# Expert weights in a ring of eight 16 KB blocks: one change to a one-core encoder step

## The chip, the cores and the metric

The kernel runs on one core of one Trainium2 chip. The metric is the time on the device, in microseconds (us), of the one core. Before the change three runs took 1047.72, 1048.99 and 1050.06 us, median 1048.99. The engines are named as in the profile: PE is TensorE, DVE is VectorE, ACT is ScalarE, POOL is GpSimd and SP is SyncE, whose queue issues most of the transfers.

## What is computed

One layer over 1104 rows (64 of a sample stream, 16 meta rows and 1024 of a prompt), model width 1024, all in 32 bit:

```python
h = x + W_out [ PoolMix(u) ; RMSNorm_head(GLA(q, k, v, alpha)) * silu(r) ]
    where [u, q, k, v, r, z] = RMSNorm(x) @ W_in
h = h + HierMoE(RMSNorm(h))        # top-1 group of 4, then top-2 of its 8 experts
y = RMSNorm(h)
# one expert:
h_e = silu(xb @ w_eg[e]) * (xb @ w_eu[e]); y_e = h_e @ w_ed[e]
```

GLA is a gated linear attention in chunks of 64 rows, PoolMix a mean over the last 2, 4, 8 or 16 rows. There are 32 experts. Each has three weight matrices of 2 MB (gate 1024x512, up 1024x512, down 512x1024), 201 MB together, and each is loaded once.

## The kernel before

**Tiles.** The rows, padded, are cut in nine tiles of 128 tokens. The *front* (the mixer) goes through them on PE one by one: tile 0 and tile 1 are written out, tiles 2 to 7 are a loop, and tile 8 is written out again. A tile's PE work is, in this order: z, q and k, then u, r, v (`proj_z`, `proj_qk_gate`, `proj_u`, `proj_r`, `proj_v`; products in L1422 and L1474), the pooling, the attention, and the output product of the tile before (L1543). The last tile's output product has two halves, and each half counts up the semaphore `pe_half_out`. All weights of the front stay in one tensor, `arena`, of 24 Ki elements per partition: first `w_in` (2064 columns by 8), then `w_out`.

**Experts.** Behind the last tile the 32 experts run, each for up to 88 gathered rows. For each expert PE computes gate and up (`up`, L1713, 256 matmuls) and down (`down`, L1725 and L1732). ACT and DVE make the hidden values between them (L804, L1237 to L1243), ACT copies the result out (L809, L813), and POOL gathers rows from `hn_rows` in memory (L556) and scatters results into `pick_rows` (L567). DVE transposes the gathered rows (L1207). Experts alternate between two sets of buffers.

**Weights.** There are two sets of three weight buffers, `wg`, `wu` and `wd`, each a 16 KB block per partition of `arena`, at the places of `starts` (L212). Expert e uses set e mod 2. The buffers lie on weights of the front, so they can only be filled when these are no longer read. SP's program does that in `load_weights` (L456): the first three loads and the fourth wait for the last tile's v product (`pe_v`), the fifth for `pe_half_out` at 2 and for the last store of `hn_rows`, the sixth for the gathered rows of expert 1. From expert 2 on each load waits for the product two experts earlier that read the same block.

**Order.** The order of the work is written by hand. Each engine runs its own program, and semaphores tie them together. SP's queue is in order: a load that waits holds up all loads behind it. PE's expert code is experts 0 and 1 written out, a loop over pairs (L1763), and experts 30 and 31 written out. Behind the first tiles and next to experts 0 to 2, DVE also builds the tables of where each result row lies (`slots`, L1261), and a small copy of the last 15 pooling rows, `pool_out` (L1226), is stored; PE's up product of expert 0 waits for it, because it clears the PSUM bank.

**The tail.** When all results are in memory SP loads them back, PE and DVE add them to `h`, and the last norm is applied (L1363, L1795 to L1804).

## Time and profile before

| what | before |
|---|---|
| median of 3 runs | 1048.99 us |
| the profiled execution | 1047.59 us |
| its span | 1045.7 us |
| PE busy | 994.2 us (95%) |
| DVE busy | 561.9 us (54%) |
| ACT busy | 243.9 us (23%) |
| POOL busy | 106.1 us (10%) |
| moved by DMA | 263.23 MB, mean 252 GB/s |
| chain that ended last | PE 66%, DMA 28%, DVE 4% |

The span is the time between the first and the last instruction that the profiler saw; the execution lasts 1.9 us longer. A busy share of PE counts a matmul as busy while it is in the pipeline, so 95% is not a measure of how well PE is used. The chain goes backwards from the last instruction to what released it, and its shares add up over stages with different limits: DMA's 28% all lie in the second half. A stage has to be looked at by itself, with the windows (busy time of each engine in a stretch), the timeline of one queue, and the DMA issues of a short window, which give the time from issue to landing. The granted clock of TensorE was at its full level in all stretches of the experts.

### The profile page before, as it was taken

Reading aid. Unit: us, or ns where it says so; the run is one execution under the profiler, and the core shown is the slowest. Engines: PE = TensorE matmul, PEld = TensorE weight load, DVE = VectorE, ACT = ScalarE, POOL = GpSimd, SP = SyncE. Lnnn points to the kernel's source line nnn. Section 1 sums busy time; section 2 is a strip of 40 time slices with the busy share of each in tenths; the row PEclk is TensorE's granted clock in tenths of the full one; section 3 lists DMA queues with packets and bytes.
Section 4 is the critical chain, followed back from the end, with each engine's and each line's share of the span. In section 5 each row is a group of like instructions: output and inputs, shape, how many; then the busy total and the mean of one; then the engine's idle time right before and its main releaser. Section 6 shows DMA issues by size and latency. Waiting matters only on the chain.

```text
span 1045.7 us, 33186 instructions
## 1 busy us (share of the span) xinstructions
PE 994.2 (95%) x14570; PEld 788.2 (75%) x14570; DVE 561.9 (54%) x1283; ACT 243.9 (23%) x531; POOL 106.1 (10%) x169
## 2 busy tenths in 40 slices
PE   7999999999999999999989999999999999999976
PEld 7786868686867677748778888788787787878842
DVE  2333534444444444427976766665756657566337
ACT  2352332323232323121111111111011110111125
POOL 0110101010101010101111011011011110111000
PEclk9999999999999999999999999999999999999989
DMA  9911010100000101175999999999999999999959
GB/s 328 337 72 41 1 41 0 40 0 40 0 40 0 40 0 40 35 328 179 410 418 424 417 425 419 420 421 416 426 415 419 421 415 424 415 419 420 384 189 387
DMA packets 54293, 263.23 MB, mean 252 GB/s; under 512 B 11368, under 2 KB 13992, under 8 KB 46026
## 3 DMA queue, kind: packets, MB, share of 16 engines
q1 hardware_dynamic: 43466, 235.12, 55.2%
q0 software_dynamic: 8192, 18.06, 4.5%
q10 hardware_dynamic: 2592, 9.44, 2.2%
q8 instruction: 32, 0.52, 0.2%
q14 instruction: 11, 0.09, 0.0%
HBM read 247.11 MB, written 27.19 MB: 262 GB/s over the span
## 4 chain that ended last, share of the span: by engine, by line
PE 66%; DMA 28%; DVE 4%; issue 1%; ACT 1%; SPq 0%; DVEq 0%; POOLq 0%; ACTq 0%
DMA arena<-in_w_ed 23%; PE bank L1422 19%; PE bank L1543 11%; PE bank L1713 11%; PE bank L1725 6%; PE bank L1474 6%; PE bank L1732 4%; DMA arena<-in_w_eg 3%; PE bank L1403 2%; PE bank L1523 1%; DVE hnT L1207 1%; DMA arena<-in_w_in 1%; PE bank L1481 1%; PE bank L1540 1%; PE bank L1802 1%
## 5 line engine op out<-in xcount | busy, mean ns | idle before, releaser
L1422 PE MATMUL bank<-xnT,arena 128*128 128x128 f32 x1728 | 201.1, 277 | 3.4 <-DMA arena<-in_w_in 2.0
L1422 PEld LDWEIGHTS bank<-xnT,arena 128*128 128x128 f32 x1728 | 196.9, 193 | 5.8 <-DVE sA L950 3.5
L1713 PEld LDWEIGHTS bank<-xnT,arena 128*64 128x64 f32 x4096 | 156.7, 137 | 10.9 <-DMA arena<-in_w_eg 7.0
L1713 PEld LDWEIGHTS bank<-hnT,arena 128*64 128x64 f32 x4096 | 156.3, 137 | 9.4 <-issue 5.2
L1713 PE MATMUL bank<-xnT,arena 128*64 128x88 f32 x4096 | 160.2, 240 | 3.2 <-DMA arena<-in_w_eg 1.9
L1713 PE MATMUL bank<-hnT,arena 128*64 128x88 f32 x4096 | 159.3, 239 | 2.3 <-DVE hnT L1216 1.6
L1543 PE MATMUL bank<-arena,mixT 128*128 128x512 f32 x256 | 111.7, 593 | 0.0
L1725 PE MATMUL bank<-arena,osq 128*32 128x384 f32 (+1 forms) x768 | 85.7, 487 | 14.4 <-DMA arena<-in_w_ed 12.3
L1237 DVE TENSOR_SCALAR mixT<-mixT 128x352 f32<-128x352 f32 x32 | 12.4, 388 | 147.5 <-ACT mixT L804 147.5
L1725 PE MATMUL bank<-arena,silu_r 128*32 128x384 f32 (+1 forms) x768 | 85.7, 487 | 6.2 <-DMA arena<-in_w_ed 4.2
L1543 PEld LDWEIGHTS bank<-arena,mixT 128*128 128x128 f32 x256 | 47.9, 190 | 57.2 <-issue 57.1
L1207 DVE STREAM_TRANSPOSE hnT<-xs 32x256 f32<-32x256 f32 x192 | 83.5, 435 | 6.2
L1732 PE MATMUL bank<-arena,silu_r 128*32 128x256 f32 (+1 forms) x384 | 86.1, 380 | 0.0
L1732 PE MATMUL bank<-arena,osq 128*32 128x256 f32 (+1 forms) x384 | 85.9, 380 | 0.0
L1207 DVE STREAM_TRANSPOSE xnT<-window_work 32x256 f32<-32x256 f32 x180 | 78.2, 434 | 5.2
L1238 DVE RECIPROCAL mixT<-mixT 128x352 f32<-128x352 f32 x32 | 75.3, 2353 | 1.1
L1474 PE MATMUL bank<-arena,xnT 128*128 128x512 f32 x144 | 64.8, 592 | 0.0
L809 ACT ACTIVATE kz_v<-bank 88x384 f32<-88x384 f32 x32 | 13.8, 482 | 172.3 <-PE bank L1732 172.3
L1732 PEld LDWEIGHTS bank<-arena,osq 128*32 128x32 f32 (+1 forms) x384 | 40.0, 107 | 16.3
L1732 PEld LDWEIGHTS bank<-arena,silu_r 128*32 128x32 f32 (+1 forms) x384 | 39.9, 107 | 16.5 <-issue 0.2
L809 ACT ACTIVATE hs<-bank 88x384 f32<-88x384 f32 x31 | 13.5, 483 | 162.2 <-PE bank L1732 162.2
L530 POOL TENSOR_TENSOR window_work<-window_work 128x568 f32<-128x568 f32 x9 | 10.2, 1135 | 397.3 <-ACT window_work L677 397.3
(260 smaller groups left out, 999.4 us busy)
## 6 DMA issues: line engine op xcount, KB each, us to landing
arena<-in_w_eg SPq DMA_DIRECT2D x32, 2048.0 KB, 26.9
arena<-in_w_eu SPq DMA_DIRECT2D x32, 2048.0 KB, 27.1
arena<-in_w_ed SPq DMA_DIRECT2D x32, 2048.0 KB, 26.7
hn_rows<-hs ACTq DMA_DIRECT2D x18, 512.0 KB, 3.4
arena<-pick_rows SPq DMA_DIRECT2D x18, 512.0 KB, 10.1
arena<-in_w_in SPq DMA_DIRECT2D x3, 2048.0 KB, 12.8
arena<-in_w_out SPq DMA_DIRECT2D x1, 4096.0 KB, 13.8
out_y_prompt<-arena SPq DMA_DIRECT2D x8, 512.0 KB, 6.2
```

What stands on the lines that cost most here:

```text
L809: A(ye[b][0:BLOCK, half * OWN:(half + 1) * OWN], bank[6 + half][0:BLOCK, 0:OWN], ACT.Copy).then_inc(s["ye_ready"], 1)
L1207: ins = V.transpose(slotsT[b][q:q + TG, :, a:a + TG], by_k[:, :, q:q + TG])
L1237: moe.then(V.tensor_scalar(gs[:, 0:NH], sig[:, 0:NH], 1.0, None, ALU.add))
L1238: moe.then(V.reciprocal(gs[:, 0:NH], gs[:, 0:NH]))
L1403: return nc.tensor.transpose(out, src, ident[0:n, 0:n])
L1422: last = mm(out, w_in_sb[:, k, a:b], xnT[:, k, :], start=k == 0, stop=k == KD - 1)
L1474: last = mm(bank[6][:, :], xnT[:, k, :], w_in_sb[:, k, V0:R0], start=k == 0, stop=k == KD - 1)
L1481: last = mm(bank[4][:, g * P:(g + 1) * P], w_pool_sb[:, g, :], pooled[:, g, :], start=True, stop=True)
L1543: return mm(out[:, :], mix[:, k, :], w_out_sb[:, k, n * 512:(n + 1) * 512], start=k == 0, stop=k == KD - 1)
L1713: last = mm(out[q * SW:(q + 1) * SW, n * BLOCK:(n + 1) * BLOCK], w[:, k, m * P + q * SW:m * P + (q + 1) * SW], rowsT[b][:, k, :], start=k ...
L1725: last = mm(bank[6 + half][a:z, 0:OWN], tokens(k, g), wd[b][:, k, half * OWN:(half + 1) * OWN], start=k == 0, stop=k == KF - 1)
L1732: return mm(bank[n][STORE:STORE + z - a, c:c + REST], tokens(k, g), wd[b][:, k, 2 * OWN:D], start=k == 0 and c == 0, stop=k == KF - 1, ski ...
```

## The change

The blocks get a new layout. `arena` becomes six blocks of 16 KB per partition (6 x `EW` elements). Two more blocks are made by laying small tensors of the front into `work` and `late`, two new tensors, with `part` and `carve`. The eight blocks form a ring: piece number 3e + kind (kind 0 gate, 1 up, 2 down) goes to place (3e + kind) mod 8. Each front weight gets a block of its own (q/k, u, r, v), and `w_out` fills two blocks, one for each half of its columns.

```diff
-        arena = sb("arena", [P, KD * D_IN + KD * D])
...
-        starts = {("g", 0): 0, ("u", 0): EW, ("d", 0): 2 * EW, ("g", 1): 3 * EW, ("u", 1): KD * D_IN, ("d", 1): KD * D_IN + EW}
...
+        arena = sb("arena", [P, 6 * EW])
+        work = sb("work", [P, EW])
+        late = sb("late", [P, D + EW])
...
+        blocks = [arena[:, n * EW:(n + 1) * EW] for n in range(6)] + [work[:, :], late[:, D:]]
...
+        w_qk_sb, w_u_sb, w_r_in_sb, w_v_sb = (by_k(blocks[n]) for n in range(4))
+        w_out_sb = arena[:, 4 * EW:].rearrange("p (h k n) -> p h k n", h=2, k=KD)
...
+        ring = [blocks[n] for n in (0, 1, 2, 3, 4, 6, 5, 7)]
+        RING = len(ring)
+        KINDS = 3
...
+        AROUND = RING
...
+            return divmod(KINDS * b + kind, RING)
```

In `work` lie `one_dv`, `w_pool_sb`, `z_sb`, `qk`, `q_wide`, `k_i`, `k_dec`, `sc`, `sB`, `pooled` and `er`; in `late` lie `w_up_sb`, both router weights, `gate_work`, `sA`, `s_sample` and the windows. The rows of the experts' first lane stay in the first part of `late`.

SP's loads change as follows. `load_freed` waits, for each piece, for the reader eight pieces earlier.

```diff
+            def load_freed(t, b):
...
+                e = AROUND * t + b
+                if not (isinstance(t, int) and e < 3):
+                    sp.wait_ge(s["pe_u2"], 2 * (e - 2))
+                    load_piece(t, b, 0)
+                    sp.wait_ge(s["pe_d"], e - 2)
+                    load_piece(t, b, 1)
+                sp.wait_ge(s["pe_g"], e - 1)
+                load_piece(t, b, 2)
+
+            sp.wait_ge(s["pe_qk"], TILES)
+            load_piece(0, 0, 0)
+            sp.wait_ge(s["pe_u"], TILES)
+            load_piece(0, 0, 1)
+            sp.wait_ge(s["pe_r"], TILES)
+            load_piece(0, 0, 2)
             sp.wait_ge(s["pe_v"], TILES)
-            load_weights(0, 0)
-            load_weights(0, 1)
+            load_piece(0, 1, 0)
             sp.wait_ge(s["sA_ready"], TILES)
             for p in range(PAIRS):
-                sp.dma_start(gla_prompt[2 * p:2 * p + 2].rearrange("h k v -> (h k) v"), sA[:, p, :]).then_inc(s["outs_stored"], 16)
+                sp.dma_start(gla_prompt[2 * p:2 * p + 2].rearrange("h k v -> (h k) v"), sA[:, p, :]).then_inc(s["states_stored"], 16)
+            sp.wait_ge(s["pe_half_out"], 1)
+            load_piece(0, 1, 1)
+            sp.wait_ge(s["own_rstd_ready"], 1)
+            load_piece(0, 1, 2)
+            sp.wait_ge(rows_in[0], 16)
+            sp.wait_ge(s["pe_half_out"], 2)
+            load_piece(0, 2, 0)
+            sp.wait_ge(s["pe_router"], TILES)
+            sp.wait_ge(s["states_stored"], 16 * 2 * PAIRS)
+            load_piece(0, 2, 1)
...
-            with sp.Fori(1, NE // 2) as t:
-                for b in range(2):
-
-                    sp.wait_ge(s["pe_g"], 2 * t + b - 1)
-                    load_weights(t, b)
+            for b in range(2, AROUND):
+                load_freed(0, b)
+            with sp.Fori(1, NE // AROUND) as t:
+                for b in range(AROUND):
+                    load_freed(t, b)
```

PE's experts are written out for one turn of eight and then run in a loop of eight, so that each has a fixed place in the ring:

```diff
-            expert(0, 0)
-            expert(0, 1)
-            with pe.Fori(1, NE // 2 - 1) as t:
-                expert(t, 0)
-                expert(t, 1)
-            expert(NE // 2 - 1, 0)
-            expert(NE // 2 - 1, 1, last=True)
...
+            for b in range(AROUND):
+                expert(0, b)
+            with pe.Fori(1, NE // AROUND) as t:
+                for b in range(AROUND):
+                    expert(t, b)
```

Four smaller edits go with the layout. The output weights come in two loads and are scaled on a strided view. `pool_out` now lies in `hs`, so DVE waits for the last store of `hn_rows` before it writes there, and ACT waits for the stores of `pool_out` before it works on expert 1. The slot tables move into constants that are no longer needed, where there is room for 18 of 25 columns, so one table takes two steps.

```diff
+            dve.wait_ge(s["hn_stored"], 16 * PICKS * TILES)
             for n in range(2):
                 V.tensor_copy(pool_out[n], bank[4 + 2 * n][0:HIST, :]).then_inc(s["pool_out_ready"], 1)
...
             expert(0, 0, True)
+            act.wait_ge(s["pool_stored"], 16 * 2)
             expert(0, 1, True)
...
+                for a in range(0, EXTRA, X_PART):
+                    n = min(X_PART, EXTRA - a)
...
-            sp.dma_start(w_out_sb, w_out.rearrange("(k p) n -> p k n", p=P)).then_inc(s["w_out_in"], 16)
+            for h in range(2):
+                sp.dma_start(w_out_sb[:, h, :, :], w_out.rearrange("(k p) n -> p k n", p=P)[:, :, h * 512:(h + 1) * 512]).then_inc(piece_in[(4, 6)[h]], 16)
```

SP's queue before, from the first expert load to the loop. `in_w_eg`, `in_w_eu` and `in_w_ed` are gate, up and down weights:

```order
L458 DMA arena<-in_w_eg 128x4096 [waits pe_v]
L464 DMA arena<-in_w_eu 128x4096
L469 DMA arena<-in_w_ed 128x4x1024
L458 DMA arena<-in_w_eg 128x4096
L464 DMA arena<-in_w_eu 128x4096 [waits hn_stored,pe_half_out]
L469 DMA arena<-in_w_ed 128x4x1024 [waits rows_in1]
L476 DMA out_gla_prompt<-sA 128x128 [waits sA_ready]
L476 DMA out_gla_prompt<-sA 128x128
L478 DMA out_pool_sample<-q_wide 15x512 [waits pool_out_ready]
L479 DMA out_pool_prompt<-sc 15x512
```

The same place of SP's queue in the changed kernel. A load into `late` or `work` is one into the two new blocks:

```order
L496 DMA arena<-in_w_eg 128x4096 [waits pe_qk]
L496 DMA arena<-in_w_eu 128x4096 [waits pe_u]
L496 DMA arena<-in_w_ed 128x4x1024 [waits pe_r]
L496 DMA arena<-in_w_eg 128x4096 [waits pe_v]
L519 DMA out_gla_prompt<-late 128x128 [waits sA_ready]
L519 DMA out_gla_prompt<-late 128x128
L496 DMA arena<-in_w_eu 128x4096 [waits pe_half_out]
L496 DMA work<-in_w_ed 128x4x1024 [waits own_rstd_ready]
L496 DMA arena<-in_w_eg 128x4096 [waits pe_half_out,rows_in0]
L496 DMA late<-in_w_eu 128x4096 [waits states_stored,pe_router]
L532 DMA out_pool_sample<-hs 15x512 [waits pool_out_ready]
L532 DMA out_pool_prompt<-hs 15x512
```

The first four loads now wait for four different products instead of one, two more loads (`in_w_eg` and `in_w_eu` of expert 2) stand ahead of the `pool_out` stores, and the two `gla_prompt` stores have moved ahead of piece 4.

PE's program before, at the end of the loop over experts (L1763 is the loop, L1732 the end of an odd expert's down product, L1713 the gate product that follows):

```order
L1725 MATMUL bank<-arena,silu_r 24x384
L1732 MATMUL bank<-arena,silu_r 24x256
L1763 REGISTER_ALU
L1763 COMPARE_AND_BRANCH
L1713 MATMUL bank<-xnT,arena 64x88 [waits g_in0,eT_ready]
```

And of the changed kernel (L1829 is its loop, L1835 reads whether experts have left-over rows):

```order
L1792 MATMUL bank<-late,silu_r 24x256
L1829 REGISTER_ALU
L1829 COMPARE_AND_BRANCH
L1835 TENSOR_LOAD steer [waits slots_ready]
L1835 ISA x2
```

Before, the branch closes a body of two experts and two more are written behind it. Now it closes a body of eight; eight more stand ahead of the loop and none behind it.

## Rows read from the trace of the kernel before

**Rows 1.** Page, part 2: rate in 40 slices of 26.1 us
```profile
GB/s 328 337 72 41 1 41 0 40 0 40 0 40 0 40 0 40 35 328 179 410 418 424 417 425 419 420 421 416 426 415 419 421 415 424 415 419 420 384 189 387
```

**Rows 2.** Windows: stretch, length, PE busy, granted clock, DMA share, GB/s
```profile
485.00:560.00 75.00, 70.44 (x1518) 1.00 0.98 395
...
560.00:650.00 90.00, 90.00 (x1939) 1.00 1.01 421
...
650.00:970.00 320.00, 300.27 (x6408) 1.00 1.01 419
```

**Rows 3.** Chain in order of time: start us, us, what
```profile
598.17 9.86 PE bank L1713 x256
...
613.35 9.86 PE bank L1713 x256
...
970.18 26.65 DMA arena<-in_w_ed
...
1002.31 0.48 ACT hs L809
```

**Rows 4.** Timeline of SP's queue: start us, us, queue, line, operation, tiles
```profile
484.35 0.33 SPq L464 DMA_DIRECT2D arena<-in_w_eu  x1
...
493.82 0.38 SPq L469 DMA_DIRECT2D arena<-in_w_ed  x1
...
542.28 0.34 SPq L458 DMA_DIRECT2D arena<-in_w_eg  x1
...
552.83 0.38 SPq L469 DMA_DIRECT2D arena<-in_w_ed  x1
```

**Rows 5.** DMA issues in windows 493.8:494 and 552.8:553: size, us to landing
```profile
arena<-in_w_ed SPq DMA_DIRECT2D x1, 2048.0 KB, 8.9
...
arena<-in_w_ed SPq DMA_DIRECT2D x1, 2048.0 KB, 18.7
```

**Rows 6.** DMA queues in 485:560, 560:970 and 970:1000: packets, MB, share
```profile
q8 instruction: 11, 0.18, 0.9%
...
q14 instruction: 1, 0.01, 0.0%
...
q8 instruction: 5, 0.08, 1.1%
```

**Rows 7.** Timeline of PE, experts 0 to 4; idle time before in brackets
```profile
485.89 9.93 PE L1713 MATMUL bank<-xnT,arena 128*64 128x88 f32 x256
...
502.73 7.35 PE L1713 MATMUL bank<-hnT,arena 128*64 128x88 f32 x188 [1.60 <-DVE hnT L1216]
...
510.27 2.80 PE L1713 MATMUL bank<-hnT,arena 128*64 128x88 f32 x68 [0.18 <-issue]
...
529.35 0.77 PE L1713 MATMUL bank<-xnT,arena 128*64 128x88 f32 x14 [0.86 <-issue]
...
552.58 7.65 PE L1713 MATMUL bank<-xnT,arena 128*64 128x88 f32 x196
```

**Rows 8.** Timeline of PE, last token tile: u, r, v and output product
```profile
418.09 7.39 PE L1422 MATMUL bank<-xnT,arena 128*128 128x128 f32 x64
...
425.60 7.39 PE L1422 MATMUL bank<-xnT,arena 128*128 128x128 f32 x64
...
438.87 1.88 PE L1474 MATMUL bank<-arena,xnT 128*128 128x512 f32 x4
...
465.21 1.88 PE L1543 MATMUL bank<-arena,xs 128*128 128x512 f32 x4
```

**Rows 9.** Timeline of ACT behind the last token tile
```profile
477.28 0.20 ACT L787 ACTIVATE ss_own<-ss_own 128x1 f32<-128x1 f32 x1
...
479.79 0.90 ACTq L795 DMA_DIRECT2D hn_rows<-hs  x2
```

**Rows 10.** Timelines of ACT and DVE: output weights scaled, slot table
```profile
49.43 2.19 ACT L646 ACTIVATE arena<-arena,mix_scale 128x1024 f32<-128x1024 f32 x2
...
518.66 0.99 DVE L1282 TENSOR_TENSOR gate_work<-cst,upto 128x800 f32<-128x800 f32 x1
```

More of the change, by code:

```diff
@@ L223, in build, with part @@
         ident = con("ident")
-        one_dv = sb("one_dv", [P, P])
+        work_at = [0]
+        def part(n):
+            a = work_at[0]
+            work_at[0] += n
+            assert work_at[0] <= EW
+            return work[:, a:a + n]
+        one_dv = part(P)
         eps = sb("eps", [P, 1])
@@ L279, in build @@
         hs = sb("hs", [P, KD, P])
+        pool_out = [hs[0:HIST, 4 * n:4 * n + 4, :].rearrange("p k n -> p (k n)") for n in range(2)]
         hss = sb("hss", [P, 1])
@@ L378, in build @@
         s = {n: sem(n) for n in names}
-        g_in = [sem(f"g_in{b}") for b in range(2)]
-        u_in = [sem(f"u_in{b}") for b in range(2)]
-        d_in = [sem(f"d_in{b}") for b in range(2)]
+        piece_in = [sem(f"piece_in{n}") for n in range(RING)]
         rows_in = [sem(f"rows_in{b}") for b in range(2)]
@@ new lines, in _ @@
+            load_piece(0, 1, 1)
[7 more added lines that the diff above has]
+            load_piece(0, 2, 1)
+            sp.wait_ge(s["pool_out_ready"], 2)
+            for n, out in enumerate((pool_sample, pool_prompt)):
+                sp.dma_start(out, pool_out[n]).then_inc(s["pool_stored"], 16)
@@ L1417, in turn_x, with features @@
                     last.then_inc(s["pe_xT"], 1)
-            def features(out, a, b):
+            def features(n, w, m):
                 for k in range(KD):
-                    last = mm(out, w_in_sb[:, k, a:b], xnT[:, k, :], start=k == 0, stop=k == KD - 1)
+                    last = mm(bank[n][:, m * P:(m + 1) * P], w[:, k, m * P:(m + 1) * P], xnT[:, k, :], start=k == 0, stop=k == KD - 1)
                 return last
@@ L1471, in proj_v @@
                 if first:
-                    pe.wait_ge(s["w_v_in"], 16)
+                    pe.wait_ge(piece_in[3], 16)
                 for k in range(a, b):
-                    last = mm(bank[6][:, :], xnT[:, k, :], w_in_sb[:, k, V0:R0], start=k == 0, stop=k == KD - 1)
+                    last = mm(bank[6][:, :], xnT[:, k, :], w_v_sb[:, k, :], start=k == 0, stop=k == KD - 1)
                 if b == KD:
@@ L1542, in out_step @@
             def out_step(n, k, out, mix):
-                return mm(out[:, :], mix[:, k, :], w_out_sb[:, k, n * 512:(n + 1) * 512], start=k == 0, stop=k == KD - 1)
+                return mm(out[:, :], mix[:, k, :], w_out_sb[:, n, k, :], start=k == 0, stop=k == KD - 1)
             def project_out(j):
@@ L1715, in up, with down @@
                 return last
-            def down(b, hid_count=None):
+            def down(b, wd, hid_count=None):
                 def tokens(k, g):
```

178 lines of the change are left out of this document (92 added, 86 removed).

## The prediction

> **What bounds the kernel now.** I read the slices first, to see which resource is full in which stage. The rate row shows two stages [rows 1]: after the first 50 us the transfers all but stop for nearly 400 us while the nine token tiles run on PE, and from slice 20 on they run at 410 to 425 GB/s to the end of the experts. The windows say the same more sharply [rows 2]: 395 GB/s in 485 to 560, 421 in 560 to 650, 419 in 650 to 970, with a DMA share of about 1.00. PE is busy for the whole of 560 to 650 and for 300.27 of the 320 us after it. So the experts start with weights in hand, PE eats the store until about 650, and from there the weight queue sets the pace.
>
> The chain gives the two paces [rows 3]. While PE leads, one expert starts every 613.35 - 598.17 = 15.18 us. From 650 the chain runs through weight loads, and the last of them lands at 970.18 + 26.65 = 996.83; the last down projection then takes until ACT's copy at 1002.31, 5.5 us later. I call the 96 weight loads of 2 MB pieces 0 to 95 (gate, up, down of expert 0, and so on). Piece 17 is issued at 552.83 and takes 18.7 us, so lands at 571.5 [rows 4, 5]. From there to piece 95 it is 425.3 us for 78 pieces, 5.45 us each, 16.36 us an expert. That is DMA's pace, 1.2 us an expert slower than PE's.
>
> Where was DMA idle that could have served? After the fourth piece it waits: piece 4 is issued only at 484.35 and piece 5 at 493.82 [rows 4]. These are the gaps that the change can fill. After 996.83 nothing of it is touched: the tail from 1002.31 to the end of the span at 1045.7 stays.
>
> **The change, part by part.** *Earlier first loads.* Piece 0 now waits only for the last tile's q/k projection, piece 1 for u, piece 2 for r, piece 3 for v. These end at 418.1, 425.5, 433.0 and 440.8 [rows 8] (u starts at 418.09, r at 425.60, each for 7.39; v ends at 438.87 + 1.88). Piece 4 follows the half of the output product that ends at 465.21 + 1.88 = 467.1. Piece 5 follows ACT's last `ss_own` at 477.5 [rows 9]; pieces 6 and 7 follow the first gathered rows, about 482. Each takes 5.0 us of the queue (2.10 MB at 421 GB/s) and 8.9 us from issue to landing when it is alone [rows 5]. All eight are in by about 500; before, pieces 5 to 7 landed after that (piece 5 at 493.82 + 8.9 = 502.7).
>
> *Two more blocks.* From then on piece n waits for piece n - 8 and not n - 6. Piece 17 waits for the fourth expert's gate product, whose end freed a block at 542.28 [rows 4]. Alone it would land at 551.2. From the other side, the queue works without a pause from 477.5 on: pieces 5 to 17 (27.3 MB) and the 1 MB store, at the 385 GB/s that 2.10 MB in 5.45 us leave beside gathers and scatters, behind a start of 8.9 - 5.0 = 3.9 us, end at 554.9. I take 554, against 571.5: 17.5 us earlier. If nothing else changed, piece 95 would land at 979.3 and the end would come 17.5 us sooner.
>
> *PE becomes the other bound.* In that case PE has to keep up. It starts expert 4 at 552.58 [rows 7], and 28 experts at 15.18 us end at 977.6, just before DMA's 979.3 + 5.5 = 984.8. The slack is 7.2 us in 28 experts, 0.26 us each, so any slowing of PE counts at once.
>
> *The PE code is written out for eight experts.* This is the part I weigh most. Before, PE's loop held two experts; now eight stand ahead of the loop and its body holds eight. The instruction queue of the trace shows what that costs [rows 6]: 11 fetches of 16 KB while experts 0 to 3 ran for the first time (485 to 560), none on that queue from 560 to 970, when the loop of two repeated, and 5 for the two experts written behind it. So an expert is 2.75 fetches, and a loop of 5.5 fetches stays on the chip. A loop of 22 has not been seen here. I take it not to fit: about 88 fetches instead of 16.
>
> What does a fetch cost? PE has small holes in that stretch whose cause is "issue": 0.18 us at 510.27, 0.86 us at 529.35 [rows 7]. Experts 0 to 3 took 552.58 - 485.89 = 66.7 us, 16.67 each, 1.49 us over the loop's pace. About half of that has other names (waits for DVE, whose slot tables fall into this stretch). Lower end: nothing, since expert 0 ran its 256 products in one unbroken 9.93 us beside fetches. Upper end: the whole 1.49 us an expert. I take 0.45 us, nearest to the experts without a wait for DVE. That is 12.6 us over 28 experts. The loop now jumps back twice over 22 blocks; no row shows such a jump. Bounds are 0 and, from the 3.9 us before a lone load's data run, about 4 us each; I take 1 us each.
>
> The Trainium skill, "Runtime: NRT & Kernel Launch", section on instruction fetch mechanics, says that PE holds 128 KiB or 2048 instructions, refilled in 16 KiB blocks, mostly hidden, but that a taken branch to a block that is not held forces a fetch before execution goes on. By its size (8 blocks) a body of 22 does not fit and one of 5.5 does; the silent instruction queue in [rows 6] agrees with the latter. Its remark that there is no cache but two lines does not. "Mostly hidden" would put the time with rival A below.
>
> A fetch also takes a DMA engine: 0.9% of 16 engines over 75 us is 10.8 us, 0.98 us a fetch [rows 6]. If they are spread, 72 more are 72 x 0.98 / 16 = 4.4 us of DMA in all, which stays inside the PE line. If all were on the engine that lands last, they would add 2.7 us an expert. Pieces 6 to 17 landed beside most of those fetches in 571.5 - 502.7 = 68.8 us, 5.73 each against 5.45: 3.4 us in all, not 8 to 10. I take the spread case.
>
> *New waits and collisions at the start.* The first gathered rows and the last 1 MB store of `hn_rows` (issued at 479.79 [rows 9], landed at 484.35, when SP goes on [rows 4]) now run beside pieces 5 and 6. DVE's `pool_out` copies, and with them PE's up product of expert 0, now wait for that store; so does the gather of expert 1, as before. Sharing the engines with one stream doubles 2.5 us of store to 5: landing about 487. PE needs `pool_out` halfway through the 9.93 us from 485.89, at 490.9, so the first wait stays covered by 2 to 3 us; without that cover it costs what the store is late. The second costs about 1.5 us. The slot table that took two DVE operations of about 0.99 us [rows 10] takes four short ones, 0.3 us more. Together I take 2 us; bounds 0 and 8 (the store as late as a whole 2 MB load's 8.9 us). ACT's wait for the pool stores matters only once expert 1, started at 502.73 [rows 7], has its gate product; they land near 502 behind piece 7: nothing, and some 2 us if they came later. The output weights come in two loads with 2 KB rows. ACT scales them from 49.43 and had not waited for them [rows 10], so I take nothing; at the 328 to 337 GB/s of the first slices [rows 1] 4.2 MB would take 2 us more, which is the upper end. The front tiles are otherwise the same.
>
> **The sum.** PE: 552.6 + 2.0 + 28 x (15.18 + 0.45) + 2 x 1.0 = 994.2, against 1002.3 before. DMA: 979.3 + 4.4 + 5.5 = 989.2. PE is the later one. The gain is 8.1 us. The profiled execution took 1047.59 with a span of 1045.7, the median of the runs is 1048.99; from it, 1040.9.
>
> **The rivals.** *A, the fetches are hidden.* PE keeps 15.18 us and DMA alone ends the experts. Gain 17.5 less 0 to 2: about 1032.5. For it: expert 0 ran beside fetches without a hole. Against it: the "issue" holes and 16.67 us. *B, written-out code is slower than the queue (the other side).* Place: PE's blocks fetched through full DMA queues, and the two jumps. Break-even is (1002.3 - 554.6 - 2.0) / 28 = 15.92 us an expert, that is 0.74 us over the loop's pace. At the 16.67 of experts 0 to 3 the experts end at 1023.4, 21 us late: 1070. At 16.1 to 16.3 it is 1054 to 1060. For it: experts 0 to 3; fetches on one busy DMA engine would give the same sign. Against it: half of those 1.49 us have DVE as their cause. *C, the start loses what the store gains.* Weights beside the last store and the gathers cost 8 us before expert 1 instead of 2 and PE does not get them back: about 1047 to 1049, no change. For it: the store ran on nearly idle engines before, 479.79 to 484.35 [rows 4, 9]. Against it: pieces 6 and 7 are only issued when the first rows are in.
>
> **Chances.** Main case 0.42, A 0.25, B 0.23, C 0.10. Faster by over 0.2% (2.1 us, about what a measurement of this kernel can tell): 0.65, from the main case and A. Within 0.2%: 0.10, from C and the main case's edge. Slower: 0.25, B and a worse C. The main case's own range is 1035 to 1047. The range to hold 8 in 10 takes in A whole and B up to 16.3 us: 1029 to 1061.
>
> **What would show it.** Right: 80 to 90 instruction fetches from 485 to 1000 instead of 16; eight pieces landed by 500 and piece 17 at 551 to 557; PE at 15.5 to 15.8 us an expert with "issue" holes, few waits for `in_w_ed`; last piece at 980 to 992. A: pace 15.2, then waits for DMA from about 900. B: pace over 15.9 with the DMA share under 1. C: expert 1 starts after 507. Wrong altogether: if the instruction queue stays silent in the new loop, or a longer hole stands where the loop jumps back.

## The result and the profile after

The changed kernel is 3.3% slower: 1083.15 us (median of 4, 1081.82 to 1086.6) against 1048.84 for the kernel before (4 runs), ratio 1.0332 [1.0303, 1.0361]. I had forecast 1041, with a range from 1029 to 1061. The profiled execution is the slowest of the four, 1086.6 with a span of 1084.7. Its span is 39.0 us longer than the one before, while the medians differ by 34.3.

The page of the changed kernel, parts 1 to 4. The slices are 27.1 us wide:

```profile
PE 1013.4 (93%) x14570; PEld 800.6 (74%) x14570; DVE 563.2 (52%) x1285; ACT 243.9 (22%) x531; POOL 105.6 (10%) x169
...
GB/s 319 332 62 40 1 40 0 39 0 39 0 39 35 4 39 157 159 241 354 402 372 394 424 418 414 419 413 416 352 377 416 416 419 354 395 408 404 94 165 382
...
q8 instruction: 103, 1.69, 0.6%
...
PE 86%; DVE 5%; issue 4%; DMA 3%; SPq 1%; ACT 1%; DVEq 0%; POOLq 0%; ACTq 0%
```

DMA's 28% of the chain have shrunk to 3%. PE has most of them, and "issue" has gone from 1% to 4%. The weights start to come in slice 16, earlier than in [rows 1], but the rate in the slices 20 to 22 is lower than before, and at slices 29 and 34 there are dips that the kernel before does not have.

The fastest way to place a loss in a periodic kernel is one instruction that comes once per period. ACT's sigmoid copy does: 32 times, one per expert. These are the copies of experts 0, 15, 16 and 31 in the changed kernel's timeline of ACT (start, duration, instruction, idle before it and its releaser), and then those of experts 0 and 31 in the kernel before:

```profile
502.14 0.46 ACT L860 ACTIVATE mixT<-bank 128x352 f32<-128x352 f32 x1 [19.24 <-PE bank L1773]
...
752.77 0.46 ACT L860 ACTIVATE mixT<-bank 128x352 f32<-128x352 f32 x1 [2.93 <-PE bank L1773]
776.64 0.46 ACT L860 ACTIVATE mixT<-bank 128x352 f32<-128x352 f32 x1 [11.04 <-PE bank L1773]
...
1030.31 0.46 ACT L860 ACTIVATE mixT<-bank 128x352 f32<-128x352 f32 x1 [2.94 <-PE bank L1773]
```

```profile
491.07 0.47 ACT L804 ACTIVATE mixT<-bank 128x352 f32<-128x352 f32 x1 [7.92 <-PE bank L1713]
...
991.63 0.46 ACT L804 ACTIVATE mixT<-bank 128x352 f32<-128x352 f32 x1 [2.93 <-PE bank L1713]
```

Expert 31 is 38.7 us late, which is nearly the whole difference of 39.0 between the two profiled executions (the tail behind it takes 54.4 us, before 54.1). All 32 starts give this account, in us:

| stretch, by sigmoid copies | before | after | late by |
|---|---|---|---|
| start of expert 0 | 491.07 | 502.14 | 11.1 |
| experts 0 to 3 | 51.14 | 53.40 | 2.3 |
| 3 to 15, 12 experts | 188.47 (15.71 each) | 197.23 (16.44 each) | 8.8 |
| the steps 15-16 and 23-24, where PE's loop jumps back | 32.23 | 48.75 | 16.5 |
| the other 14 up to 31 | 228.72 (16.34 each) | 228.79 (16.34 each) | 0.1 |

Two things stand out. Before, the seven steps from expert 3 on took 15.2 to 15.6 us and those behind them 15.7 to 16.9, at DMA's pace. After, there is no stretch at PE's own 15.2: the mean is 16.4 from expert 3 on. And two single steps cost 8 us each.

**The start.** Timelines of POOL, SP and PE, the changed kernel. Below them are the windows (busy of PE, PEld, DVE, ACT, POOL, then granted clock, DMA share, GB/s):

```profile
477.29 1.16 POOL L611 DMA_INDIRECT late<-hn_rows,first_idx  x1 [24.70 <-issue]
...
477.26 0.39 SPq L496 DMA_DIRECT2D work<-in_w_ed  x1
487.05 0.33 SPq L496 DMA_DIRECT2D arena<-in_w_eg  x1
487.47 0.57 SPq L496 DMA_DIRECT2D late<-in_w_eu  x1
...
502.07 0.41 SPq L496 DMA_DIRECT2D arena<-in_w_ed  x1
...
487.17 1.98 PE L1745 MATMUL bank<-cst,late 88*128 88x88 f32 x8 [5.76 <-DMA late<-hn_rows,first_idx]
...
490.82 3.62 PE L1754 MATMUL bank<-cst,hs 128*128 128x88 f32 x16
...
494.92 11.96 PE L1773 MATMUL bank<-xnT,arena 128*64 128x88 f32 x256
```

```profile
482.00:487.00 5.00, 0.00 (x0) 0.00 (x0) 0.65 (x6) 0.39 (x3) 0.00 (x0) 0.85 1.00 347
487.00:491.00 4.00, 3.83 (x19) 3.87 (x20) 1.59 (x9) 0.00 (x0) 0.00 (x0) 0.50 1.07 389
491.00:495.00 4.00, 4.00 (x23) 3.94 (x24) 1.31 (x4) 0.00 (x0) 0.00 (x0) 0.50 0.98 414
495.00:500.00 5.00, 5.00 (x80) 5.00 (x82) 1.88 (x8) 0.00 (x0) 1.99 (x2) 0.58 0.96 381
500.00:505.00 5.00, 5.00 (x138) 5.00 (x136) 2.33 (x2) 0.46 (x1) 0.00 (x0) 1.00 0.57 163
```

Piece 5 (`work<-in_w_ed`) is issued 0.03 us before the gather of the first rows. This gather had no weight load beside it before; now it takes 9.74 us instead of 3.9 (changed kernel, chain; kernel before, DMA issues of 477 to 481, last column us to landing):

```profile
477.29 9.74 DMA late<-hn_rows,first_idx
```

```profile
window_work<-hn_rows,first_idx POOLq DMA_INDIRECT x1, 3.9
```

PE stands still for 5.76 us, and the granted clock falls to 0.50, the lower level of 1.2 GHz, until about 499: eight products of L1745 take 1.98 us instead of 1.10 (L1685 before), the 256 products of expert 0 take 11.96 instead of 9.93 [rows 7]. The idle time costs 5.8 us, the clock most of the rest of 11.1.

**The two long steps and the small holes.** Timeline of PE at expert 16, at expert 24, and the group row of one of the two gate and up forms (busy, mean ns of one, idle before it):

```profile
768.04 3.97 PE L1773 MATMUL bank<-xnT,arena 128*64 128x88 f32 x60 [4.56 <-issue]
773.73 5.07 PE L1773 MATMUL bank<-xnT,arena 128*64 128x88 f32 x128 [1.71 <-issue]
779.93 2.80 PE L1773 MATMUL bank<-xnT,arena 128*64 128x88 f32 x68 [1.13 <-issue]
...
906.26 4.67 PE L1773 MATMUL bank<-xnT,arena 128*64 128x88 f32 x60 [4.50 <-issue]
911.94 9.40 PE L1773 MATMUL bank<-xnT,arena 128*64 128x88 f32 x196 [1.01 <-issue]
```

```profile
L1773 PE MATMUL bank<-xnT,arena 128*64 128x88 f32 x3072 | 129.8, 248 | 17.2 <-issue 17.2
```

Both long holes stand at the first product of an expert where PE's loop starts over, and smaller ones follow them, as the next blocks of code come in. The holes are not the whole price. The clock falls behind them too, as two windows of the changed kernel show (clock in the third place from the end):

```profile
769.00:772.00 3.00, 3.00 (x42) 2.87 (x39) 0.00 (x0) 0.00 (x0) 0.76 (x2) 0.50 0.96 397
906.00:914.00 8.00, 6.73 (x89) 6.60 (x91) 0.00 (x0) 0.00 (x0) 1.23 (x2) 0.50 0.90 376
```

At the full clock 256 of these products take 9.93 us [rows 7], so 60 take 2.3 and 196 take 7.6. Of the 8.7 us by which the step of expert 16 is longer than 15.18, the three holes are 7.4 and the clock is about 1.6 (3.97 instead of 2.3). Of the 9.7 us at expert 24 the holes are 5.5 and the clock is about 4.1 (4.67 and 9.40 instead of 2.3 and 7.6).

The waits of the changed kernel from 485 to 1040 hold "PE bank L1773 <- issue: 34.5, 32, 4.6" and no wait of PE for `in_w_ed`. Before, in 500 to 1000, the order was the reverse (line, releaser: us in total, times, longest):

```profile
PE bank L1725 <- DMA arena<-in_w_ed: 16.5, 17, 1.6
...
PE bank L1713 <- issue: 1.4, 4, 0.9
```

The wait for weights has been exchanged for one that the profile calls "issue". That it is a wait for code is what the experiments have to show.

### The profile page after: what moved, and what is told of

It reads as the page before. It is cut to its first block, busy times and chain, and to the rows that moved or that the text cites. A ratio compares the mean times of both kernels' runs of the same rounds, so it can differ in the third digit from the quotient of the medians.

```text
span 1084.7 us, 33099 instructions
## 1 busy us (share of the span) xinstructions
PE 1013.4 (93%) x14570; PEld 800.6 (74%) x14570; DVE 563.2 (52%) x1285; ACT 243.9 (22%) x531; POOL 105.6 (10%) x169
## 4 chain that ended last, share of the span: by engine, by line
PE 86%; DVE 5%; issue 4%; DMA 3%; SPq 1%; ACT 1%; DVEq 0%; POOLq 0%; ACTq 0%
PE bank L1773 30%; PE bank L1482 18%; PE bank L1603 11%; PE bank L1785 9%; PE bank L1534 6%; PE bank L1792 5%; DVE hnT L1264 2%; PE bank L1463 1%; DMA arena<-pick_rows 1%; PE bank L1583 1%; DMA late<-hn_rows,first_idx 1%; PE bank L1541 1%; PE bank L1600 1%; DMA late<-in_w_gate_up 1%; SPq L559 1%
## 5 line engine op out<-in xcount | busy, mean ns | idle before, releaser
L1773 PE MATMUL bank<-xnT,arena 128*64 128x88 f32 x3072 | 129.8, 248 | 17.2 <-issue 17.2
L1773 PEld LDWEIGHTS bank<-xnT,arena 128*64 128x64 f32 x3072 | 125.6, 143 | 25.0 <-issue 24.9
L1773 PE MATMUL bank<-hnT,arena 128*64 128x88 f32 x3072 | 124.2, 240 | 14.9 <-issue 13.3
L1773 PEld LDWEIGHTS bank<-hnT,arena 128*64 128x64 f32 x3072 | 119.4, 137 | 20.9 <-issue 18.3
L1785 PE MATMUL bank<-arena,osq 128*32 128x384 f32 (+1 forms) x768 | 88.2, 495 | 2.9 <-DVE osq L1301 1.9
L1264 DVE STREAM_TRANSPOSE xnT<-late 32x256 f32<-32x256 f32 x180 | 78.2, 434 | 5.2
L585 POOL TENSOR_TENSOR late<-late 128x568 f32<-128x568 f32 x9 | 10.2, 1132 | 397.1 <-ACT late L732 397.1
L860 ACT ACTIVATE mixT<-bank 128x352 f32<-128x352 f32 x32 | 14.8, 463 | 135.1 <-PE bank L1773 130.5
L1534 PEld LDWEIGHTS bank<-arena,xnT 128*128 128x128 f32 x144 | 26.0, 191 | 25.8 <-issue 25.8
L1792 PE MATMUL bank<-arena,silu_r 128*32 128x256 f32 (+1 forms) x192 | 43.3, 380 | 0.0
## 6 DMA issues: line engine op xcount, KB each, us to landing
arena<-in_w_in SPq DMA_DIRECT2D x4, 2048.0 KB, 13.4
```

The costliest lines, as they stand in the source:

```text
L860: A(sig[:, 0:NH], bank[2 + b][:, 0:NH], ACT.Exp, scale=-1.0).then_inc(s["sig_ready"], 1)
L1264: ins = V.transpose(slotsT[b][q:q + TG, :, a:a + TG], by_k[:, :, q:q + TG])
L1534: last = mm(bank[6][:, :], xnT[:, k, :], w_v_sb[:, k, :], start=k == 0, stop=k == KD - 1)
L1773: last = mm(out[q * SW:(q + 1) * SW, n * BLOCK:(n + 1) * BLOCK], w[:, k, m * P + q * SW:m * P + (q + 1) * SW], rowsT[b][:, k, :], start=k ...
L1785: last = mm(bank[6 + half][a:z, 0:OWN], tokens(k, g), wd[:, k, half * OWN:(half + 1) * OWN], start=k == 0, stop=k == KF - 1)
L1792: return mm(bank[n][STORE:STORE + z - a, c:c + REST], tokens(k, g), wd[:, k, 2 * OWN:D], start=k == 0 and c == 0, stop=k == KF - 1, skip_g ...
```

## The experiments

Theory 1: PE's code, written out beyond what stays on the chip, is fetched through DMA engines that the weights keep full, and this costs about 1.2 us an expert and the 8 us steps. Theory 2, for the start: piece 5 collides with the first gather. Rivals: the new ring itself (its waits, its blocks in `work` and `late`), or a cost of written-out code or of jumps that has nothing to do with DMA. The results in one table, with the sigmoid accounts; ratios are to the kernel before in the same job. The columns from "expert 0" on are read from the one profiled execution of each kernel. Thin, half and small8 do not compute the layer and ran once each:

| kernel | us (n) | ratio [95%] | expert 0 | 3 to 15, each | two steps | other 14, each |
|---|---|---|---|---|---|---|
| before | 1048.84 (4) | 1 | 491.07 | 15.71 | 32.2 | 16.34 |
| after | 1083.15 (4) | 1.0332 [1.0303, 1.0361] | 502.14 | 16.44 | 48.8 | 16.34 |
| code8 | 1073.75 (4) | 1.0246 [1.0224, 1.0268] | 492.48 | 16.20 | 49.2 | 16.21 |
| late5 | 1077.65 (4) | 1.0280 [1.0260, 1.0299] | 492.08 | 16.30 | 49.1 | 16.27 |
| ring6 | 1043.54 (4) | 0.9949 [0.9932, 0.9965] | 492.62 | 15.18 | 31.9 | 16.31 |
| ring6b | 1045.76 (10) | 0.9977 [0.9963, 0.9991] | 492.17 | 15.18 | 31.9 | 16.32 |
| code32 | 1062.53 (4) | 1.0130 [1.0111, 1.0149] | 492.95 | 16.38 | 32.2 | 16.59 |
| code4 | 1087.32 (4) | 1.0367 [1.0331, 1.0402] | 490.36 | 17.15 | 47.2 | 16.72 |
| thin | 1036.59 (1) | - | 491.91 | 15.18 | 36.8 | 15.17 |
| half | 1042.35 (1) | - | 493.10 | 15.26 | 41.4 | 15.28 |
| small8 | 1089.18 (1) | - | 490.48 | 17.13 | 49.1 | 16.80 |
| ring8_32 | 1058.06 (4) | 1.0100 [1.0073, 1.0127] | 493.28 | 16.23 | 32.1 | 16.18 |
| plus2 | 1046.74 (10) | 0.9987 [0.9975, 0.9999] | 490.75 | 15.38 | 31.3 | 16.19 |
| early5 | 1054.89 (5) | 1.0063 [1.0042, 1.0083] | 502.24 | 15.18 | 32.2 | 16.29 |

The step columns are sums over experts 15-16 and 23-24, whatever the kernel does there (code4 has other jumps inside its two averages).

**code8: the code alone.** The kernel before, with its old buffers and loads. Only PE's experts are written out for eight and looped by eight.

```diff
-            expert(0, 0)
-            expert(0, 1)
-            with pe.Fori(1, NE // 2 - 1) as t:
-                expert(t, 0)
-                expert(t, 1)
-            expert(NE // 2 - 1, 0)
-            expert(NE // 2 - 1, 1, last=True)
+            for n in range(PER):          # PER = 8
+                expert(0, n)
+            with pe.Fori(1, NE // PER) as lap:
+                for n in range(PER):
+                    expert(lap, n)
```

> The kernel before with one edit: PE's expert code is written out for eight experts and then runs in a loop of eight, as in the changed kernel; blocks, loads and waits stay as before. Theory 1 (PE's instruction stream is what costs: each expert's code is fetched anew, about 1.2 us an expert and some 8 us at each of the two jumps back): the experts need 28 x 16.4 + 16 us from expert 4 on, so 1070 to 1076 us, 85 to 90 fetches on the instruction queue, and the 'issue' holes of the changed kernel. Theory 2 (the ring of eight blocks or its waits cost the time, the code is free): 1049 us, no change. Theory 3 (only the collision at the start costs): 1049 us as well.

24.6 us slower, with the two long steps (25.0 and 24.2) at the same experts and 82 instruction fetches from 485 to 1000. The longest hole is the first product of expert 16:

```profile
754.26 4.20 PE L1713 MATMUL bank<-xnT,arena 128*64 128x88 f32 x60 [5.61 <-issue]
```

```profile
q8 instruction: 82, 1.34, 1.0%
```

So the code is the larger part of the loss, without any new ring.

**late5: piece 5 behind the first rows.** The changed kernel with one line moved.

```diff
             sp.wait_ge(s["own_rstd_ready"], 1)
-            load_piece(0, 1, 2)
             sp.wait_ge(rows_in[0], 16)
+            load_piece(0, 1, 2)
```

> The changed kernel with piece 5 (the down weights of expert 1) issued behind the first gathered rows instead of beside their gather. Theory of the start collision: the first gather lands 4 us after its issue instead of 9.8, PE has no hole of 5.8 us and TensorE's granted clock stays at 2.4 GHz ahead of expert 0, whose products start at 486 to 487 instead of 494.9; the time falls by 8 to 10 us, to 1073 to 1075. Rival (PE is bound by its instruction stream and catches up nothing, but the gather was slow for another reason, such as its rows being stored late): the gather stays at 9 to 10 us and the time at 1083.

Expert 0 is back at 492.08, with the clock at 1.00 throughout. But the time falls by 5.5 us only, where I had expected 8 to 10. The gather of expert 1's rows now stands behind three weight loads. The chain of late5 shows it:

```profile
488.15 11.14 DMA xs<-hn_rows,idx_i
```

PE waits 2.64 us behind these rows (1.60 in the changed kernel), and experts 0 to 3 take 56.6 us instead of 53.4. The collision was moved to the next gather, for a third of its price.

**ring6: early loads and a ring, with the loop of two.** The changed kernel with a ring of only the six blocks of `arena`, so that the places repeat every two experts. The two early loads for expert 2 go, and each later load waits for the reader six pieces earlier (that part of the edit is not shown).

```diff
-        ring = [blocks[n] for n in (0, 1, 2, 3, 4, 6, 5, 7)]
+        ring = [blocks[n] for n in range(6)]
-        AROUND = RING
+        AROUND = 2
...
-            sp.wait_ge(s["own_rstd_ready"], 1)
-            load_piece(0, 1, 2)
             sp.wait_ge(rows_in[0], 16)
             sp.wait_ge(s["pe_half_out"], 2)
-            load_piece(0, 2, 0)
-            sp.wait_ge(s["pe_router"], TILES)
-            sp.wait_ge(s["states_stored"], 16 * 2 * PAIRS)
-            load_piece(0, 2, 1)
+            load_piece(0, 1, 2)
```

> The changed kernel with a ring of the six arena blocks, so that PE's loop holds two experts again; the early first loads stay (pieces 0 to 4 as in the changed kernel, piece 5 behind the first gathered rows and the second output half). If the instruction stream is the cause of the loss: 16 to 20 fetches, PE at 15.2 us an expert, and the early loads give what the depth of the queue allows: piece 6 lands near 500 instead of 508.4, the last piece near 986 instead of 996.8, 1037 to 1041 us. If early loads are worth nothing (DMA catches up anyway, or the collisions at the start eat them): 1047 to 1050. If the new layout itself costs (packing of small tensors, two loads of w_out): above 1052.

1043.54 us, 0.9949 [0.9932, 0.9965], with no instruction fetch on q8 in 560 to 970 (only "q14 instruction: 1, 0.01, 0.0%"). The last piece lands at 992.75 instead of 996.8. I had expected 986, and 1037 to 1041 us. The early loads were worth this much less, once the code repeated. It is also the control for theory 1, in its window from 560 to 700:

```profile
560.00:700.00 140.00, 140.00 (x3048) 121.37 (x3046) 93.76 (x173) 22.65 (x55) 22.55 (x38) 1.00 1.02 421
```

With the engines full and no code to fetch, PE keeps 15.18 us an expert.

**code32 and code4: is it the jump or the code?** code8 with `PER` 32 (no jump back at all) and with `PER` 4 (four written out, a loop of four, a body of about 10 to 11 blocks).

> The kernel before with all 32 experts of PE written out and no loop. In the kernel with a loop of eight the trace shows 16.3 us an expert and two experts of 24 to 25 us where PE's loop jumps back. If a jump back costs by itself (about 8.6 us each): 1055 to 1058 us and no expert above 18 us. If the long experts are only the stream catching up (the same bytes have to come anyway): 1070 to 1075 us. In both cases the instruction queue shows about 85 fetches from 485 to 1000.

> The kernel before with four experts written out and a loop of four, a body of about ten 16 KB blocks, with six jumps back. If a body of ten blocks does not stay on the chip and a jump costs 8.6 us: some 85 fetches, 16.3 us an expert and 24 to 25 us at experts 8, 12, 16, 20, 24 and 28: 1103 to 1110 us. If jumps are cheap: 1055 to 1060. If it does stay: 20 to 25 fetches, 15.2 us an expert until DMA is the bound, 1049 to 1051.

The waits of code32, 500 to 1000, and its queue, 485 to 1000:

```profile
PE bank L1713 <- issue: 20.7, 27, 2.0
```

```profile
q8 instruction: 80, 1.31, 1.0%
```

Without a jump no step behind expert 3 is over 17.8 us, and the pace of 16.4 stays: two separate costs. The time lies between the two forecasts, 1055 to 1058 and 1070 to 1075. The two jumps were worth 1073.75 - 1062.53 = 11.2 us (from two jobs), less than the two steps' excess of 16 to 17, since the other steps are longer here, 16.38 and 16.59 against 16.20 and 16.21. In code4 every fourth step takes 22.9 to 23.8 us, and the two experts behind each jump but the first take 15.2 to 15.5. It has 86 fetches ("q8 instruction: 86, 1.41, 1.1%"), so a body of 10 to 11 blocks is not kept either. Its time is 1087.32 and not the 1103 to 1110 that I expected of its six jumps, for a like reason: behind a jump the steps are shorter. The window behind the jump at 695 fits theory 1, since the weight queue has worked off part of its loads while PE waited:

```profile
698.00:718.00 20.00, 19.86 (x434) 17.69 (x432) 10.00 (x19) 2.46 (x6) 1.13 (x2) 0.97 0.91 344
```

**thin and half: empty the DMA engines.** late5, but from expert 3 on only the first part of each weight block is loaded: 1/8, 1/8 and 1/4 in thin, half in half. The rest of each block keeps old values, so the results are not the layer's.

```diff
-                sp.dma_start(weights(b, kind), src).then_inc(piece_in[place(b, kind)[1]], 16)
+                k = slice(0, (KF if kind == 2 else KD) if isinstance(e, int) and e < 3 else 1)
+                sp.dma_start(weights(b, kind)[:, k, :], src[:, k, :]).then_inc(piece_in[place(b, kind)[1]], 16)
```

> The changed kernel with piece 5 late and, from expert 3 on, only the first of a weight block's four or eight row groups loaded (0.25, 0.25 and 0.5 MB instead of 2 MB each); the other weights of a block are those of an earlier expert, so the experts' results are not those of the reference. The PE code and all waits stay. It tells whether the holes of PE's instruction stream come from full DMA queues. If they do: 'issue' holes shrink to a few us in all, an expert takes 15.2 to 15.4 us, each jump back costs 2 to 4 us, 1035 to 1045 us. If the holes are the sequencer's own (block edges and jumps cost the same on idle queues): 16.3 us an expert and 8 us a jump, 1070 to 1075 us.

> The changed kernel with piece 5 late and, from expert 3 on, half of each weight block loaded (the rest stays that of an earlier expert, so the results are not those of the reference). With all bytes an expert takes 16.4 us, with a seventh of them 15.2. If holes come when a fetch meets a loaded DMA engine: in between, by the share of time that the queues are busy (about half), 15.5 to 15.9 us an expert, jumps of 4 to 6 us, 1048 to 1058 us. If only full queues hurt: 15.2 to 15.3 us, as with a seventh.

The windows 560 to 960 of thin, of half and of the changed kernel, in this order:

```profile
560.00:960.00 400.00, 395.56 (x8508) 341.55 (x8506) 262.86 (x494) 63.07 (x154) 60.33 (x102) 1.00 0.36 106
```

```profile
560.00:960.00 400.00, 391.58 (x8414) 338.68 (x8411) 257.51 (x480) 63.83 (x156) 60.31 (x102) 0.99 0.73 239
```

```profile
560.00:960.00 400.00, 370.07 (x7651) 313.70 (x7647) 238.23 (x450) 56.57 (x138) 54.65 (x92) 0.98 0.99 402
```

The code is the same, and thin still fetches ("q8 instruction: 90, 1.47, 1.2%" in 485 to 1000). PE's pace goes to 15.2 at a DMA share of 0.36 and to nearly the same, 15.3, at 0.73. Only at 0.99 is it 16.3. The two long steps fall in turn, from 23.8 and 25.3 in late5 to 19.7 and 21.7 and to 17.8 and 19.0. Together with ring6 this says that the small holes need both, code that is fetched and full DMA engines. A jump has a price at any load: 2.6 to 3.8 us over 15.2 at 0.36, 4.5 to 6.5 at 0.73, and 7.5 to 9 over 16.3 at full load. The clock is part of the higher prices: at expert 24 of half the 256 products behind the 3.80 us hole take 12.56 us instead of 9.93, and in thin the clock stays at 1.00. Of my two forecasts for half, the pace between, 15.5 to 15.9, was wrong and the other, 15.2 to 15.3, right.

**small8: shorter packets.** code8 with gate and up weights loaded in rows of 2 KB per packet instead of the whole 16 KB row of a partition; the weights land in another order of the contraction, so the results are not the layer's.

```diff
-                sp.dma_start(wg[b], w_eg[bass.ds(e * D, D), :].rearrange("(p k) n -> p k n", k=KD)).then_inc(g_in[b], 16)
+                sp.dma_start(wg[b], w_eg[bass.ds(e * D, D), :].rearrange("(k p) n -> p k n", k=KD)).then_inc(g_in[b], 16)
```

> The kernel with a loop of eight on the old blocks, with gate and up weights loaded in rows of 2 KB instead of 16 KB for each partition (other rows of the matrix land in a partition, so the experts' results are not those of the reference; bytes and waits are the same). If an instruction block waits behind the large packets of each DMA engine: the 'issue' holes shrink from 29 us to under 12, 15.3 to 15.7 us an expert. If it waits for the bytes queued whatever their packets: holes as before, 16.3 us. If the small rows make the weight queue slower: waits for in_w_eg instead.

If a fetch waited for the large packets ahead of it, small packets should have helped it. They didn't: the hole at expert 16 is still 4.72 us, PE's holes of "issue" make 33.6 us from 485 to 1040 (29.4 in code8), and the rate falls from 411 to 389 GB/s (560 to 960). The first forecast failed. The second, holes as before, came true, and of the third so much that PE also waits 14.2 us for weights, and the pace is 17.1 and 16.8 and not 16.3. How a fetch and the weights share an engine stays open.

**ring8_32: does the stock of eight blocks get used?** late5 with all 32 experts of PE written out.

```diff
-            for b in range(AROUND):
-                expert(0, b)
-            with pe.Fori(1, NE // AROUND) as t:
-                for b in range(AROUND):
-                    expert(t, b)
+            for b in range(NE):
+                expert(0, b)
```

> The changed kernel (eight blocks) with piece 5 late and all 32 experts of PE written out, so without a jump. The same code on the old six blocks took 1062.5 us, with 16.3 us an expert from the fourth on. If written-out code is pulled to the pace of the full weight queue whatever is in stock (its instruction blocks come through the same engines): again 16.3 us an expert although no load is waited for, 1056 to 1062 us; two more blocks are worth nothing but the few us of the earlier start. If the extra stock lets PE run at 15.2 us for longer: 1045 to 1050.

PE never waits for weights here, and its pace is 16.2 all the same, as the first forecast has it. Pieces 17 and 95 (size, us to landing), and the first down products of expert 31:

```profile
arena<-in_w_ed SPq DMA_DIRECT2D x1, 2048.0 KB, 16.2
...
late<-in_w_ed SPq DMA_DIRECT2D x1, 2048.0 KB, 30.8
```

```profile
1007.17 0.52 PE L1785 MATMUL bank<-late,silu_r 128*32 128x384 f32 x3
```

Piece 17 lands at 565.20, 20.7 us before PE starts on it, and piece 95 at 1001.09, 6.1 us before. So the stock is used, but only by 14.6 us in 26 experts, 0.56 us each. PE's own pace of 15.2 would have used it up in about 13 experts (an estimate, from 1.6 us an expert). The weight queue is slower as well, although no load that I read was in sooner than 16 us, against 8.9 for one alone: 435.9 us for these 78 pieces, 16.77 us an expert, against 425.3 before and 424.5 in ring6. That leaves little for two more blocks to buy: 1.0100 against the 1.0130 of code32, in another job and with intervals that overlap.

**plus2: two more blocks, once.** ring6 with two extra blocks in `work` and `late` for gate and up of expert 2, and four experts written out ahead of the loop of two.

> The ring of six with its loop of two, and the two new blocks used once, for gate and up weights of expert 2, which are issued right behind piece 5 at about 483; four experts are written out ahead of the loop. If the time is set by how much DMA has done before the engines fill for good at about 495: 2 to 4 us less than the ring of six (1043.5), so 1039 to 1042. If the earlier loads only collide with the gathers of experts 1 and 2 and the longer written-out part: 1043 to 1046.

1046.74 against 1045.76 of ring6b in the same job: no gain, my 1039 to 1042 was wrong. PE's own pace lasts two experts longer, but expert 1 is late (20.6 us instead of 16.8), piece 17 lands at 569.74 (ring6 568.29) and the last piece at 994.97 (992.75). So what the extra loads store is lost again ahead of piece 17; how much of it the gathers cost, and how much the two more experts written out, was not separated.

**early5: the collision alone.** ring6 without one wait, so that piece 5 is issued at 477.51, as in the changed kernel.

```diff
-            sp.wait_ge(rows_in[0], 16)
```

> The ring of six with piece 5 issued as soon as its block is free (about 475.5), so that it runs beside the first gather, as in the changed kernel. If that collision is what delays expert 0: the gather takes 7 to 10 us instead of 4, PE stands still for 4 to 6 us, the granted clock falls to 0.5 behind it, expert 0 starts 6 to 9 us later. Of these the end of the kernel shows 4 to 8 us (1048 to 1051), since the weight queue, which is the bound at the end, also starts its next piece later. If the gather is slow for another reason: no difference, 1043.5.

9.1 us slower than ring6b in the same job, and expert 0 starts 10.1 us later, both more than the 4 to 8 and 6 to 9 that I had expected. Timeline of PE and two windows of early5:

```profile
488.12 1.59 PE L1738 MATMUL bank<-cst,late 88*128 88x88 f32 x8 [4.41 <-DMA late<-hn_rows,first_idx]
```

```profile
487.00:495.00 8.00, 6.88 (x36) 6.92 (x37) 2.38 (x11) 0.00 (x0) 0.00 (x0) 0.60 0.23 92
495.00:500.00 5.00, 5.00 (x83) 4.94 (x83) 2.40 (x8) 0.00 (x0) 2.00 (x2) 0.62 0.30 77
```

DMA is at 0.23 and 0.30 of its share there, and PE is busy, yet the clock stays low: the second half of the loss is the clock's and not the transfers'. Two microseconds between load and gather did not save the gather (8.4 us instead of 3.9).

**ring6b** is ring6 once more, beside the last three.

> The ring of six once more, beside the two variants on the same chip: 1042 to 1045 us.

0.9977 [0.9963, 0.9991]: faster than before, by 2.3 us where the first job gave 5.6. The ring of six is the fastest version that computes the layer.

The parts, priced one by one, nearly make the whole: code 24.6 (code8) + start 9.1 (early5) - early loads 2.3 (ring6b) = 31.4 of 34.3 us. The sum is support and no proof, since the parts were priced in different kernels: in early5 the DMA engines stand nearly idle from 491 to 495 (share 0.02), which the changed kernel avoids with pieces 6 and 7. The other 3 us were not separated.

## Why the prediction was wrong

**Reading of the bounds: right.** ring6 shows the two paces that I read, 15.18 while PE leads and 16.31 once DMA is the bound.

**Pieces earlier: right in kind.** All eight pieces were in at 500.67. Piece 17, forecast for 554, landed at 566.65, 5 us earlier than before instead of 17.5: expert 0 came 11.1 us late, the experts up to 3 another 2.3, and with them the products that free its block. ring6's early loads, without the late start, landed the last piece 4 us earlier.

**The written-out code: this step failed, as a term of the sum.** I had the body as too large for the chip, 88 fetches, and 0.45 us an expert with an upper end of 1.49. The trace has 79 fetches from 485 to 1000 and 86 to 1040. The cost was 16.39 - 15.18 = 1.2 us an expert (26 experts from 3 on without the two steps). The step that failed is the choice of 0.45 out of experts 0 to 3 [rows 2, 7]. It spread their loss over four experts and asked what a fetch costs, not when. The trace of the kernel before had the answer, in two windows and in the second wait for DVE:

```profile
490.00:495.00 5.00, 5.00 (x138) 5.00 (x136) 3.33 (x4) 0.47 (x1) 0.00 (x0) 1.00 0.66 238
500.00:510.00 10.00, 8.40 (x206) 7.68 (x199) 9.46 (x22) 2.46 (x6) 3.26 (x4) 1.00 1.03 421
```

```profile
531.69 0.52 PE L1725 MATMUL bank<-arena,osq 128*32 128x384 f32 x3 [1.57 <-DVE osq L1243]
```

Expert 0, my witness for free fetches, ran in part at a DMA share of 0.66; from 500 on the engines were full. Of the 66.7 - 4 x 15.18 = 6.0 us the waits for DVE are 1.60 + 1.57. The other 2.8 belong to experts 1 to 3, 0.9 each by this estimate, twice what I took. With the measured 1.21 us instead of 0.45 this term alone was 21 us too small, three times the 7.2 us of slack that I had given PE.

**The jumps: this step failed too.** I priced them at 1 us, between 0 and 4, from the 3.9 us before a lone load's data. They cost 8 us each, outside my bounds. The bound was from an idle queue. Even at a full one the hole before the first product is 4.5 us, little more than the bound. What I left out comes behind it: smaller holes of 1.0 to 2.8 us in all, and a clock at 0.50 that costs 1.6 and 4.1 us.

**The start: this step failed.** Two us taken, 8 as the bound, 13.4 measured (11.1 up to expert 0, 2.3 more to expert 3). I named the first gathered rows as running beside piece 5, but priced only the store of `hn_rows`; the gather starts 0.03 us after piece 5 and took 9.74 us. And I had no price for the clock that falls behind PE's idle time. What made the 2.3 us up to expert 3 was not separated; ring6 and code32, without the collision, have 1.7 and 1.9 of them.

With the measured terms the prediction's own sum comes out: 552.6 + 13.4 + 28 x 16.39 + 2 x 8.0 = 1040.9, and ACT's last expert copy starts at 1040.48. That is bookkeeping and no test of its own, since the terms are taken from the same trace. Rival B (16.1 to 16.3 us an expert: 1054 to 1060) was the mechanism, with C's collision on top. Each was foreseen, their sum was not: as I wrote them they excluded each other.

**DMA's line: the fetch right, its effect too small.** A fetch took 1.0% of 16 engines x 515 us / 79 = 1.04 us of one engine, near the 0.98 from before. But I took 4.4 us for all of them, and in ring8_32, whose queue is never empty, the 78 pieces from 17 to 95 take 10.7 us longer than before, 0.41 us an expert. That is more than the spread case and far from the 2.7 us of one engine alone. It did not decide the changed kernel, where no product waits for weights: it was the wait of PE that mattered.

**Written out or looped.** For the effect first: code32, all written out and without a jump, is 1.3% slower than the loop of two, and thin, at a DMA share of 0.36, loses nothing to fetches ahead of a jump. The Trainium skill, "Runtime: NRT & Kernel Launch", section "Instruction fetch mechanics", calls the cost of crossing a 16 KiB boundary "mostly hidden" and says that kernels prefer full unrolling, since a taken branch outside what is held forces a fetch. The second half agrees with the steps of 8 us here. The first half agrees at a DMA share of 0.36 and 0.73 and not at 0.99. Full unrolling costs 14.8 us in this kernel (code32, 1062.53 against 1047.76 in the same job), where the body of two is kept.

## What to carry to other kernels

Count the blocks of code of a loop body before you lengthen it: where the short body repeats without instruction fetches and the DMA engines are full, code that has to be fetched costs PE its lead, and each jump several microseconds. Extra stock for a DMA-bound stage helps only if the consumer can really run faster than the transfers while they run at full rate. And an early load of 2 MB must not be issued just ahead of a small gather that the critical engine waits for: price the gather behind it, and the clock after the idle time too.

## What the runs showed of the hardware

- A loop of two experts (about 5.5 blocks of 16 KB) repeats without instruction fetches, bodies of 10 to 11 and of about 22 blocks do not. Nothing between was tried.
- Between jumps, fetched code cost PE time only beside full DMA engines: 15.2 to 15.3 us an expert at shares of 0.36 and 0.73 (one run each), 16.2 to 16.4 at 0.99 to 1.01, and 15.18 at 1.02 without fetches. How a fetch and the weights share an engine stays open.
- With fetches, a weight queue that was never empty landed 78 pieces of 2 MB in 435.9 us (ring8_32), without them in 424.5 and 425.3 (ring6, before).
- A jump over code that is not held costs 2.6 to 3.8 us at a share of 0.36, 4.5 to 6.5 at 0.73 and 7.5 to 9 at full load. In the changed kernel 1.6 and 4.1 us of it are the clock at 0.50 behind holes of 4.5 us.
- A gather of rows took 3.9 us with no weight load beside it, 8.4 to 9.7 beside one load of 2 MB, and 11.1 behind three.
- After an idle time of 4.4 to 5.8 us the granted clock was at 0.50 for another 10 us (early5) and 12 us (changed kernel) with PE busy again.
- With gate and up weights in packets of 2 KB instead of 16 KB the rate was 389 instead of 411 GB/s (small8, one run, against code8).
